# One list of sixteen latent and forget-gate tiles in a round of attention, in place of eight and eight

## The reference

```python
s = jnp.einsum('bhqd,bhkd->bhqk', qi, k) * scale
if log_decay is not None:                # the forget-gate kind
    s = s + c[..., :, None] - c[..., None, :]
p = jax.nn.softmax(jnp.where(mask, s, lowest), axis=-1)
o = jnp.einsum('bhqk,bhkd->bhqd', p, v)
```

## Time and profile before

| | us |
|---|---|
| median of 3 runs | 2896.94 (2895.53 to 2898.58) |
| the profiled execution | 2896.24 |
| its span, first to last instruction | 2894.4 |
| TensorE busy | 2699.8 (93%) |
| VectorE, ScalarE, GpSimd busy | 1095.2, 631.0, 386.1 |
| mean granted clock of TensorE | 0.972 |
| stage B, first scores to output projection | 384.2 to 693.1 |

### The profile page before, as it was taken

How to read it: one execution, slowest core, us unless ns; L and a number is a source line. 1 busy time by engine, 2 the same in 40 slices (tenths; PEclk the granted TensorE clock), 3 DMA queues, 4 the chain that set the end, 5 groups by cost and what they waited for, 6 DMA issues and landing times.

```text
span 2894.4 us, 53992 instructions
## 1 busy us (share of the span) xinstructions
PE 2699.8 (93%) x19156; PEld 2303.3 (80%) x19157; DVE 1095.2 (38%) x2700; ACT 631.0 (22%) x1387; POOL 386.1 (13%) x382
## 2 busy tenths in 40 slices
PE   7999998888989998679999999999999999999994
PEld 5444456565467776579999999999999999999994
DVE  1111145553211221633333334344445454454543
ACT  0233345552011111111111111111111212112122
POOL 0000021222000000201111111111112111111212
PEclk9999999999989999789999999999999999999997
DMA  7111242214020000745566667777788888888863
GB/s 274 37 51 51 63 138 59 64 46 155 37 88 15 14 13 16 282 170 196 195 222 218 239 230 269 266 272 259 277 301 296 297 293 294 294 303 284 304 245 133
DMA packets 97194, 525.29 MB, mean 181 GB/s; under 512 B 23968, under 2 KB 46432, under 8 KB 72544
## 3 DMA queue, kind: packets, MB, share of 16 engines
q1 hardware_dynamic: 76352, 490.60, 46.1%
q0 software_dynamic: 20768, 33.65, 5.6%
HBM read 501.92 MB, written 56.85 MB: 193 GB/s over the span
## 4 chain that ended last, share of the span: by engine, by line
PE 88%; DVE 4%; issue 3%; ACT 2%; DVEq 1%; ACTq 1%; POOLq 1%; DMA 0%; POOL 0%; SPq 0%
PE bank L1146 52%; PE wide L1533 18%; PE wide L1146 8%; PE bank L1139 4%; PE wide L1252 2%; PE bank L1483 2%; DVE biased L1758 1%; PE wide L1269 1%; PE bank L1308 1%; DVE prob_t L1769 1%; ACT st_q L956 1%; DVE low L1749 0%; ACTq L911 0%; ACT prob L976 0%; POOLq L690 0%
## 5 line engine op out<-in xcount | busy, mean ns | idle before, releaser
L1146 PE MATMUL bank<-xe_t,slot 128*128 128x128 f32 (+4 forms) x8192 | 1030.4, 288 | 33.9 <-issue 33.8
L1146 PEld LDWEIGHTS bank<-xe_t,slot 128*128 128x128 f32 x8192 | 1020.8, 193 | 36.4 <-issue 36.2
L1533 PE MATMUL wide<-act_t,slot 128*128 128x128 f32 (+4 forms) x4096 | 517.5, 287 | 0.0
L1533 PEld LDWEIGHTS wide<-act_t,slot 128*128 128x128 f32 x4096 | 507.9, 191 | 2.7 <-issue 1.8
L2029 DVE TENSOR_SCALAR glu<-bank,b_gu 128x256 f32<-128x256 f32 x256 | 123.9, 484 | 779.7 <-PE bank L1146 779.7
L1097 ACT ACTIVATE sig<-glu 128x256 f32<-128x256 f32 x256 | 106.7, 417 | 849.9 <-DVE glu L2029 847.5
L1146 PE MATMUL bank<-w_in,xt 128*128 128x512 f32 (+1 forms) x512 | 216.7, 579 | 3.8 <-DVEq L1677 3.8
L1104 ACT ACTIVATE y_t<-wide,b_dn 128x256 f32<-128x256 f32 x256 | 107.3, 470 | 440.0 <-PE wide L1533 440.0
L811 POOL DMA_INDIRECT xg<-d_xn,gidx x66 | 68.3, 1034 | 928.5 <-DVEq L1959 892.1
L1146 PEld LDWEIGHTS bank<-w_in,xt 128*128 128x128 f32 x512 | 96.8, 192 | 111.3 <-issue 110.7
L848 POOL DMA_INDIRECT share<-d_gate,sidx x64 | 67.6, 1056 | 453.8 <-DVEq L2048 443.8
(11 more groups left out here) (271 smaller groups left out, 2312.6 us busy)
## 6 DMA issues: line engine op xcount, KB each, us to landing
slot<-in_w_gu SPq DMA_DIRECT2D x128, 2048.0 KB, 7.8
slot<-in_w_dn SPq DMA_DIRECT2D x64, 2048.0 KB, 7.6
w_in<-in_w_in SPq DMA_DIRECT2D x1, 6144.0 KB, 25.3
w_mem_k<-in_w_mem_kv SPq DMA_DIRECT2D x1, 4096.0 KB, 12.9
w_mem_v<-in_w_mem_kv SPq DMA_DIRECT2D x1, 4096.0 KB, 22.5
x_sb<-in_x SPq DMA_DIRECT2D x8, 512.0 KB, 3.6
cneg<-d_cneg SPq DMA_DIRECT2D x8, 512.0 KB, 6.7
w_o<-in_w_o SPq DMA_DIRECT2D x1, 4096.0 KB, 18.6
```

The costliest lines, as they stand in the source:

```text
L1146: m = pe.matmul(dst, l, r_, start=(k == 0), stop=(k == n - 1))
L1533: x = pe.matmul(pp2[b][:, (m % 2) * CAP:(m % 2) * CAP + w], slots[4 + m // 4][:, k, (m % 4) * P:(m % 4 + 1) * P], act_t[:, k, 0:w], start= ...
```

## The change

The two halves of a round become one list: (0, 6), (0, 0), (0, 5), (1, 7), (0, 1), (1, 6), (0, 2), (1, 5), (0, 3), (1, 4), (0, 7), (1, 0), (0, 4), (1, 1), (1, 2), (1, 3). Steps 3, 5, 7 and 9 are long forget tiles with short latent ones between. `B_ROWS` becomes 13 and 15, as the last latent tile is step 12. All first and last steps of a kind are taken from the list (`B_FIRST`, `B_LAST`). Two orders inside a step differ besides. With a forget tile in hand and a latent one next, scores of the next go ahead of each head's transposes, and `row_low` ahead of each head's copy, where before both came after. With two forget tiles in a row VectorE does both `row_low` and then both copies, where before they alternated. `prob_t` gets four full buffers, and `low`, `rs`, `rr` and `rr_row` move to addresses that later stages use.

```diff
-        B_TILES = [6, 0, 7, 1, 5, 2, 4, 3]
-        B_PAIRS = [(y, i) for y in range(2) for i in B_TILES]
-        B_ROWS = (NT, NP - 1)
+        B_PAIRS = [(0, 6), (0, 0), (0, 5), (1, 7), (0, 1), (1, 6), (0, 2), (1, 5), (0, 3), (1, 4), (0, 7), (1, 0), (0, 4),
+                   (1, 1), (1, 2), (1, 3)]
+        B_FIRST, B_LAST = ([f([p for p, pair in enumerate(B_PAIRS) if pair[0] == y]) for y in range(2)]
+                           for f in (min, max))
+        B_ROWS = (B_LAST[0] + 1, B_LAST[1])
...
                 for y in range(2):
-                    po.wait_ge(b_ot, NP * h + NT * (y + 1))
+                    po.wait_ge(b_ot, NP * h + B_LAST[y] + 1)
                     apart(po)
                     values_of(h + 1, y)
                     normalise(h, y)
...
                     for a_ in range(2):
+                        if nxt and not pair and y == 1:
+                            scores(*nxt, a_)
                         turned(h, p, a_)
                         if nxt and not pair and y == 0:
-                            scores(*nxt, a_)
-                    if nxt and not pair and y == 1:
-                        for a_ in range(2):
                             scores(*nxt, a_)
...
                     if p == B_ROWS[0]:
                         inverse(h, 0)
+                    if pair and y == 1:
+                        for a_ in range(2):
+                            row_low(*nxt, a_)
                     for a_ in range(2):
-                        if pair and y == 1:
+                        if nxt and not pair and y == 1:
                             row_low(*nxt, a_)
                         turned_copy(h, p, a_)
                         if nxt and not pair and y == 0:
                             row_low(*nxt, a_)
                     if p == B_ROWS[1]:
                         inverse(h, 1)
-                    if nxt and pair != (y == 1):
+                    if pair and y == 0:
                         for a_ in range(2):
                             row_low(*nxt, a_)
                     if p in B_ROWS:
                         inverse_row(h, B_ROWS.index(p))
```

More of the change, by code:

```diff
@@ L136, in build @@
         spent_end = keep.at
+        lg_at = keep.at
         lg = keep("lg", [P, NT, E])
@@ L202, in build @@
         r = Region(15, 31)
-        prob_t = [[r(f"prob_t{s_}{a_}", [P, NT >> s_, P]) for a_ in range(2)] for s_ in range(2)]
-        assert r.at <= a_end
-        r.at = a_end
-        low = r("low", [P, 4 * NT])
-        rs = r("rs", [P, 4 * NT])
-        rr = r("rr", [P, 4 * NT])
-        r = Region(27, 28)
-        assert r.at >= base + 15 * 1024 + 3 * NT * P * 4
-        rr_row = [r(f"rr_row{y}", [2 * NT, P]) for y in range(2)]
+        prob_t = [[r(f"prob_t{s_}{a_}", [P, NT, P]) for a_ in range(2)] for s_ in range(2)]
+        low, rs, rr = (nc.alloc_sbuf_tensor_at(n, [P, 4 * NT], F32, offset=w_r_at + 4 * P + 16 * NT * k)
+                       for k, n in enumerate(("low", "rs", "rr")))
+        rr_row = [nc.alloc_sbuf_tensor_at(f"rr_row{y}", [2 * NT, P], F32, offset=lg_at + 4 * P * y) for y in range(2)]
         r = Region(159, 167)
```

22 lines of the change are left out of this document (11 added, 11 removed).

## The result

| | before | after |
|---|---|---|
| median, us | 2897.76 (4 runs) | 2925.52 (4 runs, 2924.91 to 2926.13) |
| ratio, 95% interval | 1 | 1.0097 (1.0079 to 1.0114) |
| span of the profiled execution | 2894.4 | 2923.0 |
| first transposes of (0, 6) to output projection | 304.61 | 328.03 |
| from there to the end of the span | 2201.32 | 2206.39 |

The account below looks back on a forecast made before the run. TensorE was taken as busiest, with its gaps to be won. Rounds and projection start gave +15.1 us, the clock +3.0: +18, a median of 2915 us, range 2896 to 2926.

Parts of the forecast that it names:

- The third thing that moves: Row-sum inversions go from after steps 7 and 15 to steps 13 and 15; VectorE then stands about 3 us.
- T: Time from a round's start, the first transposes of (0, 6), to its first `rr_row` copy; forecast 66.2 us.
- the chain: From first `rr_row` copy through DMA round trip and GpSimd's three passes to `b_all.free`: 13.65 us, bounds 13.4 to 14.5.
- Rival (2): At VectorE's second `rr_row` copy, `b_all.free` is already given: +4.4 us, 2901, no change; chance 0.13 with neighbouring cases.
- The first term: Steps 0 to 13: how far the new order gets by the first `rr_row` copy, 66.2 us.
- The walk: Hand timing of the sixteen steps at traced prices, without clock falls; some 10 us of TensorE gaps before step 14.
- the new wait: VectorE's second `rr_row` copy waits for GpSimd's `b_all.free`, about 3 us; TensorE then stands about 2 us.
- The second term: End of the three full rounds, behind the first `rr_row` copy: round 79.7 us against 76.5, +9.6 in all.
- The third term: Last round: projection waits at the barrier for GpSimd's `normalise(3, 0)`, starting at 80.6 us against 75.1, +5.5.
- The fourth term: Clock falls at restarts: 1.0 us for each of three rounds, 0 at the projection with a bound of 2.
- Rival (1): Attention rounds: long forget tiles' gaps fill with latent scores; at T = 58 -18 us, 2879; chance 0.12.

Follow-up runs that it names:

- number 9: Changed kernel with the 64 copies to `o_t` made by VectorE at the end of each step instead of ScalarE: 2930.17 us, ratio 1.0114.
- 7: Changed kernel with ScalarE's copy of tile p - 2 to `o_t` placed between the next step's two heads: 2932.50 us, ratio 1.0121.
- number 3: Changed kernel with values of the tiles of steps 1 and 11 multiplied six times over to keep TensorE busy: 2924.31 us, ratio 1.0097.
- number 5: Changed kernel with VectorE alternating `biased` and copy again for two forget tiles in a row (steps 13 and 14): 2925.34 us, ratio 1.0091.
- number 1: Changed kernel with the second `rr_row` copy no longer waiting for the round's first `normalise`: 2923.12 us, ratio 1.0094.
- Number 8: Changed kernel with edits of number 1 and number 5, forget reciprocal at step 15's start, GpSimd arriving at the barrier before its last latent pass: 2911.31 us, 1.0044.
- 11: Changed kernel with the edits of number 1 and number 5 together and no other: 2919.01 us, ratio 1.0071.
- Number 4: Changed kernel's code and in-step orders with the old list of eight and eight: 2919.34 us, ratio 1.0080.

## Why the prediction was right, and where its size was off

**The third thing that moves, the row sums: right.** All four second copies start at the end of GpSimd's `square`, 13.49 to 14.53 us behind the first; the range given was 13.4 to 14.5. The round is T + 13.8, where T + 13.5 was forecast and, with 1.0 for the clock, rounds of 80.7; they are 82.5, 82.8 and 81.8. In the rows that the chain was taken from, the prediction read all eight times from copy to first multiply as 6.42 to 7.55; one is 6.40 and the last round's second is 8.21 (691.37 to 699.58). Rival (2), the wait hidden, is out: 1.0 to 4.3 us in every round.

**The first term: T came at 68.2 in the mean, not 66.2.** That is four times 2.0, so 8 of the 10 us that were missing. The walk holds to step 3, which TensorE enters at 3.1, 7.9 and 12.5 for steps 1 to 3 against 3.0, 7.8 and 12.4. Step 4 is entered at 20.8 instead of 19.4: the one step that the prediction told in full is the one that failed. TensorE in step 3, after:

```profile
402.41 0.70 PE L1250 MATMUL wide<-k_mla,q_mla 96*128 96x256 f32 x2 [1.24 <-DVE low L1755]
...
403.83 1.11 PE L1137 MATMUL bank<-const,prob 128*128 128x128 f32 x8 [0.66 <-ACTq L978]
...
405.85 0.65 PE L1137 MATMUL bank<-const,prob 128*128 128x128 f32 x4 [0.42 <-ACTq L978]
...
407.35 0.66 PE L1137 MATMUL bank<-const,prob 128*128 128x128 f32 x4 [0.86 <-ACT prob_t L986]
```

and ScalarE beside it:

```profile
403.84 0.38 ACT L986 ACTIVATE prob_t<-bank 128x256 f32<-128x256 f32 x1 [0.16 <-issue]
404.45 1.15 ACT L974 ACTIVATE prob<-biased,low 128x1024 f32<-128x1024 f32 x1 [0.23 <-issue]
...
406.24 0.28 ACT L995 ACTIVATE o_t<-bank 128x128 f32 x1 [0.55 <-issue]
406.70 0.60 ACT L986 ACTIVATE prob_t<-bank 128x512 f32<-128x512 f32 x1 [0.18 <-issue]
```

Two copies had been left out of ScalarE's queue. The second `prob_t` copy of the tile before (0.38, with its gaps 0.6) stands between the two exponents, so head 1 may be turned at 17.3 from the round's start and not at 16.7. Then `b_out` (0.28, with the gaps 1.0 from the row sum's end to the next start) stands before the copy that frees bank 1, and TensorE waits 0.86 where 0.2 was allowed. In number 9, with `b_out` out of ScalarE's queue, that wait is gone and step 4 is entered 0.7 us earlier, which bears this out; the kernel got slower all the same in 7 and 9, so the work has no cheaper place in either. Steps 5 to 8 lose 0.6 more in the same way; from step 8 to T the walk is some 0.4 off in all. The mean T of 68.2 is above the 67.5 that made the top of the range, so it is in part luck that 2925.5 lies below 2926.

**T is not all of it: the clock belongs in the walk.** "My walk has no fall in it" was said of the walk and priced only at the restarts behind the new wait. Most falls came elsewhere: behind the stands of 1.1 to 1.2 in step 3 (rounds 2 to 4) and around those of 1.7 ahead of the latent sums (all rounds). At the end of a round there was one in round 1 only, and one at the projection. The count of 0 to 6 us for all clock loss was far too low for TensorE's busy time (+15.3). How much of that reached the sum is not settled: most of the low clock lies in steps 13 to 15, where TensorE's path runs beside the chain. Numbers 3 and 5 removed falls there and gained nothing, while VectorE's wait for GpSimd grew.

**The second term: right in size, its picture half right.** Gaps of 13.5 us and a start at T + 13.8 are as worked out. But VectorE was to wait 3 us and TensorE to stand 2 us at the second group of (0, 6). VectorE waited 2.6, 1.1 and 1.0, and the list of TensorE's waits has none there in any round. TensorE's own path through steps 13 to 15 was longer than the walk's by the low clock. Its gap without the wait was taken as 10.8; number 1 shows 11.0 without a fall and 12.9 with one, and in numbers 8 and 11, with the shorter stand ahead of the latent sums, it is mostly 9.6 to 10.1. So the prediction named one path and its length correctly, but not how near the second lies. It put that 3 us shorter; in rounds 2 and 3, with the low clock, it is only 0.6 to 0.7 us shorter, which is why so little is won without the wait.

**The third term: right.** The projection started at T + 13.96 (T + 14.4). TensorE stood 3.4 us in front of it, where the prediction named 5 as the sign.

**The fourth term: the clock at the projection was taken as 0, bounded by 2; behind the projection's start 5.1 us were lost, most of it to the clock.** After, the groups behind the barrier:

```profile
716.61 10.00 PE L1144 MATMUL bank<-w_o,o_t 128*128 128x512 f32 x16 [3.38 <-DVEq L380]
```

and before:

```profile
693.08 7.13 PE L1146 MATMUL bank<-w_o,o_t 128*128 128x512 f32 x16 [0.72 <-ACTq L382]
```

2.9 us are lost in the first sixteen matmuls alone. Another low stretch follows 26 us later:

```profile
742.50:750.00 7.50, 7.09 (x19) 4.16 (x19) 1.77 (x4) 0.00 (x0) 3.13 (x2) 0.54 0.66 220
```

against one of 4 us at 717.5 before, at the same place of the program. The sixteen matmuls there, after and before:

```profile
744.93 9.48 PE L1144 MATMUL wide<-w_o,o_t 128*128 128x512 f32 x16 [0.41 <-issue]
```

```profile
717.82 8.75 PE L1146 MATMUL wide<-w_o,o_t 128*128 128x512 f32 x16 [0.41 <-issue]
```

From the projection's start to their end it is 37.8 us against 33.5, so 4.3 of the 5.1 are lost by then; where the last 0.8 went was not looked at. The bound of 2 came from a restart that cost 1.0, with the clock low for some 3.5 us; here it is low for 7, TensorE works 5.9 of them, and half of that is the 2.9 lost. The Trainium skill, TensorE: Matmul & The Clock Gate, Part 1, has the throttled state as the default and activity releasing it; the trace agrees at the projection, where the clock is low behind the 3.4 us stand, and the 10.00 us row prices it higher than the 2 us that were read from the rule for all places together. No run here shows why the stand of step 3 has a fall behind it in rounds 2 to 4 and none in round 1.

**Rival (1), a better weave: out, and for the stated reason.** The gaps of the forget half that scores had caused did go (19.1 to 9.6 us), as the diff promised. Others came for them, on the same VectorE and on ScalarE. The Trainium skill, Perfetto Trace Analysis, Optimization Strategy, holds that interleaving regimes with different contended engines may improve performance; the windows show TensorE as the busiest in both halves and the result is +28 us, so its condition was not met. Number 4 adds what no step of the prediction had asked: the new order inside a step costs 22 us by itself with the old list. The prediction looked at it in step 13, and the new list has two forget tiles in a row only in steps 13 and 14, where the chain hides much of it.

**What stays open.** How much of 28 us the falls cost in the end is not settled, since in every experiment that removed some another path moved up. Number 8 gives back 14 us; what the other 14 are made of was not taken apart. The low stretch some 25 us behind the projection's start is 4 us long before, 7 in after, 3 to 7 in the other runs, and absent in the profiled executions of numbers 1 and 3. Why is not shown. Behind the projection's start after takes 4 us longer than number 1 (2206.4 against 2202.4), as much as most of the edits are worth, so a difference of a few us between two profiled spans is not proof of an edit's effect.

## What to carry to other kernels

Before interleaving two kinds of work, look at what each kind does once at its end: here a store, a load and three passes of GpSimd, 13.5 us, had 33 to 42 us until the next were due, and the weave put both ends into the last three steps. When a wait is removed and nothing is won, look for a second path of nearly the same length before dropping the theory, and remove both in one run: 2.4 and 0.2 us of the median alone, 6.5 together. In a hand walk of in-order queues put down every instruction of every engine, the small copies too, and cost the walk once more with the clock low behind stands of the length that has falls behind it in your own traces (here 1.1 us and more).

## What was not expected of the hardware

- The granted clock fell to 0.50 around stands of 1.1 to 1.75 us with TensorE at work for 85% of the stretch, in eight places of the four rounds (one of them behind 2.3 us); number 5's stand of 0.86 ahead of the latent sums had none behind it. Length alone doesn't tell: before has 13 stands of over 1 us in the four rounds and three falls, after has 16 and eight. In round 1 of after the 1.24 us stand of step 3 had none and the 1.74 us stand ahead of the latent sums had one; in number 1 it was the other way round, with the clock low from 404 to 407.5 and 1.00 around 456. Where it falls changes between like executions.
- What a low stretch costs differs: 1.0 us for 3.5 us among small matmuls with waits between the earlier trace rows, 2.9 us for the 5.9 us of work in the 7 us at the projection's first sixteen of 512 columns (10.00 against 7.13).
- Removing low clock can be worth nothing: in number 3 the mean granted clock of the four rounds went from 0.95 to 0.97 and their time stayed at 328.03 us.
